# A hybrid decoder step on one core: the second layer's mixing four turns later, its loads left where they are

## The reference

```python
for l in range(DEPTH):                                   # DEPTH = 2
    sp, ss = adaln(c_prompt, ...), adaln(c_sample, ...)  # shift, scale, gate of each sub-layer
    hp = modulate(rmsnorm(xp, norm_mix[l]), sp[0], sp[1])
    if l % N_MIXERS == 0:
        mp, r_p = mla_prompt(hp, ...)                    # attention over the prompt
        ms, r_s = mla_sample(hs, pos_s, cache_mla[i], page_table, ...)   # 16 cached pages a sequence
    else:
        mp, st_p = pool_mixer(hp, zero_prefix, pos_p, w_pool[i], pool_scale[i])  # trailing means, a map
    xp = xp + sp[2][:, None, :] * mp
    hp = modulate(rmsnorm(xp, norm_ffn[l]), sp[3], sp[4])
    xp = xp + sp[5][:, None, :] * peer(hp, ...)          # and the same for the samples

def peer(h, w_q, subkeys, u, v):                         # per token, 8 heads
    s = einsum(q, subkeys); vals, idx = lax.top_k(s, 16) # two sides of 128 keys
    best, ci = lax.top_k(vals0 + vals1, 16)              # 16 of 256 pairs -> 16 experts of 16384
    a = gelu(einsum('td,tkd->tk', x, u[e]))
    return einsum('tk,tkd->td', softmax(best) * a, v[e])
```

## Time and profile before

| | |
|---|---|
| median of 3 runs | 3481.03 us (3477.01 to 3484.01) |
| the profiled execution: its own time | 3478.81 us |
| its span in the trace | 3477.0 us |
| mean granted TensorE clock | 0.883 |
| PE busy | 2769.2 us (80%) |
| DVE busy | 2276.8 us (65%) |
| ACT busy | 1038.8 us (30%) |
| POOL busy | 1211.8 us (35%) |
| read from HBM | 1260.46 MB, 364 GB/s over the span |

### The profile page before, as it was taken

One profiled execution on the slowest core, in us unless ns is written; L12 is line 12 of the kernel. 1 busy time (PEld: TensorE's weight loads), 2 busy tenths in 40 slices (PEclk: granted clock), 3 DMA queues, 4 the chain that ended last, 5 costly groups with the idle time before them and its releaser, 6 DMA issues.

```text
span 3477.0 us, 39434 instructions
## 1 busy us (share of the span) xinstructions
PE 2769.2 (80%) x11227; PEld 1231.0 (35%) x11227; DVE 2276.8 (65%) x6373; ACT 1038.8 (30%) x4428; POOL 1211.8 (35%) x1077
## 2 busy tenths in 40 slices
PE   4988889979889957988989769979875775666765
PEld 0345554434444423434434234434331232112321
DVE  1454558887877856777777576777776645565455
ACT  0222224424334412433435314434421111111111
POOL 0000014433333423443434334434444344444443
PEclk9989999989999978999999979999988677777777
DMA  9650049999999998999999989999999999999998
GB/s 338 253 207 24 13 182 406 407 364 409 376 375 413 404 354 358 416 401 408 409 397 410 417 337 414 412 405 419 403 391 411 410 422 409 421 406 372 421 421 353
DMA packets 201876, 1266.40 MB, mean 364 GB/s; under 512 B 23762, under 2 KB 44803, under 8 KB 61874
## 3 DMA queue, kind: packets, MB, share of 16 engines
q0 software_dynamic: 150784, 1091.03, 76.9%
q1 hardware_dynamic: 50873, 172.85, 13.1%
HBM read 1260.46 MB, written 3.79 MB: 364 GB/s over the span
## 4 chain that ended last, share of the span: by engine, by line
PE 40%; DMA 29%; DVE 15%; issue 7%; ACT 3%; POOL 2%; SPq 1%; DVEq 0%; POOLq 0%; ACTq 0%; PEldq 0%
PE bank L1106 15%; DMA ring<-in_uv,work 10%; DMA big<-in_uv,work 8%; DMA mod_mix<-in_uv,work 7%; PE bank L844 6%; PE bank L956 5%; DVE ring L1946 2%; DMA ring<-in_w_ada 2%; PE bank L861 2%; PE bank L790 2%; ACT work L1425 1%; PE bank L660 1%; PE bank L617 1%; PE bank L691 1%; POOL ring L1464 1%
## 5 line engine op out<-in xcount | busy, mean ns | idle before, releaser
L1106 PE MATMUL bank<-ring,work 128*64 128x512 f32 (+1 forms) x2080 | 909.3, 710 | 276.6 <-ACT work L1425 276.2
L1464 POOL DMA_INDIRECT ring<-in_uv,work x520 | 608.8, 1171 | 944.5 <-PE bank L1106 818.8
L1946 DVE CUSTOM_DVE_ANT_0 ring<-ring,mod_smp 128x1024 f32<-128x1024 f32 x512 | 622.3, 1224 | 273.2 <-DMA ring<-in_uv,work 266.4
L1413 ACT ACTIVATE work<-work 128x2 f32<-128x2 f32 x520 | 105.2, 202 | 1509.9 <-DVE work L1946 1509.6
L1464 POOL DMA_INDIRECT big<-in_uv,work x260 | 299.6, 1152 | 682.8 <-PE bank L1106 367.9
L844 PE MATMUL bank<-big 128*128 128x512 f32 x1024 | 512.1, 623 | 0.0
L1106 PE MATMUL bank<-big,work 128*64 128x512 f32 (+1 forms) x1040 | 317.7, 730 | 152.8 <-ACT work L1425 152.6
L1106 PEld LDWEIGHTS bank<-ring,work 128*64 128x64 f32 (+1 forms) x2080 | 211.2, 153 | 627.7 <-ACT work L1425 387.5
L1946 DVE CUSTOM_DVE_ANT_0 big<-big,mod_smp 128x1024 f32<-128x1024 f32 x256 | 309.8, 1224 | 138.9 <-DMA big<-in_uv,work 135.0
L1106 PE MATMUL bank<-work 128*64 128x512 f32 (+1 forms) x520 | 293.8, 693 | 93.6 <-ACT work L1425 93.5
L1425 ACT ACTIVATE work<-small,work 128x64 f32<-128x64 f32 (+1 forms) x1040 | 303.2, 339 | 145.2 <-DVE work L1956 139.1
(11 more groups left out here) (289 smaller groups left out, 3404.2 us busy)
## 6 DMA issues: line engine op xcount, KB each, us to landing
big<-in_wk SPq DMA_DIRECT2D x48, 1152.0 KB, 10.1
ring<-in_w_ada SPq DMA_DIRECT2D x64, 768.0 KB
work<-in_cache_mla SPq DMA_DIRECT2D x104, 160.0 KB, 8.9
ring<-in_uv,work POOLq DMA_INDIRECT x520, 11.8
big<-in_uv,work POOLq DMA_INDIRECT x260, 12.1
ring<-in_w_mla_out SPq DMA_DIRECT2D x1, 4096.0 KB, 13.0
big<-in_w_mla_out SPq DMA_DIRECT2D x4, 1024.0 KB, 11.6
mod_smp<-in_cache_mla SPq DMA_DIRECT2D x24, 160.0 KB, 12.7
```

Of the source, the lines that this page charges most:

```text
L1106: last = mm(out, diag[:, t % 2, j, 0:min(m, HALF)], s[:, D + half * 512:D + (half + 1) * 512], start=(k == 0 and (n < S0 or j == 0)), stop ...
L1413: act.activation(acts[:, t % 2 * GRP:(t % 2 + 1) * GRP], dots[:, t % 2 * GRP:(t % 2 + 1) * GRP], ACT.Gelu)\
L1464: pool.indirect_dma_start(slot[g % SLOTS], None, T["uv"].rearrange("l e d -> (l e) d"), bass.IndirectOffsetOnAxis(index[:, k * GRP + j:k * ...
L1946: dve.tensor_tensor_reduce(u, u, hb, 1.0, 0.0, ALU.mult, ALU.add, dots[:, at:at + 1]).then_inc(sem("dots_set"), 1)
```

## The change

Three numbers per pair are raised. The mixing (`mix_at`) and the norms after it (`norm_turn`) stand four turns later: 132 and 260, 140/142 and 268/270. The queries and the ranking of pairs 2 and 3 (`head_turn`) stand five turns later, and the loads of these pairs' first two heads (`t == opens + 12`) four. The loads of `mods` and `pooling_weights` keep their turns, since they are now counted from `opens` and not from `mix_at`. What is computed and what is loaded stays the same.

```diff
--- before.py
+++ after.py
@@ -289,7 +289,7 @@
         tile_of = lambda n: n % NT if n < S0 else NT
 
         def head_turn(q, h):
-            return (8 * h - 12 if h else -20, 54 + 9 * h, opens[2] + 19 + 12 * h, opens[4] + 19 + 12 * h)[q]
+            return (8 * h - 12 if h else -20, 54 + 9 * h, opens[2] + 24 + 12 * h, opens[4] + 24 + 12 * h)[q]
 
         PART_AT = ((0, 1, 2, 3, 4, 5, 6, 7), (0, 1, 2, 3, 4, 5, 7, 8), (0, 1, 2, 5, 6, 7, 10, 11), (0, 1, 2, 5, 6, 7, 10, 11))
         PARTS = ((0, 0), (0, 1), (0, 2), (1, 0), (1, 1), (1, 2), (0, 3), (1, 3))
@@ -306,9 +306,9 @@
         def rank_no(n, h):
             return n // 2 * 16 + h * 2 + n % 2 if n < S0 else 64 + n - S0
 
-        norm_turn = {0: -34, 1: -33, 2: 40, 3: 41, 4: opens[2] + 8, 5: opens[2] + 10, 6: opens[4] + 8, 7: opens[4] + 10,
+        norm_turn = {0: -34, 1: -33, 2: 40, 3: 41, 4: opens[2] + 12, 5: opens[2] + 14, 6: opens[4] + 12, 7: opens[4] + 14,
                      S0: smp_open[S0] + 2, S1: smp_open[S1] + 2}
-        mix_at = {4: opens[2], 6: opens[4]}
+        mix_at = {4: opens[2] + 4, 6: opens[4] + 4}
         ybank = lambda i: pb[4:6]
 
         busy = set(range(41, 46))
@@ -494,7 +494,7 @@
                         if h >= 2 and t == head_turn(q, h - 2) - 2:
                             sp.wait_ge(sem("sco_ps"), i - 1)
                             load_head(q // 2, i, h)
-                        if q and h < 2 and t == (40, opens[2] + 8, opens[4] + 8)[q - 1] + h:
+                        if q and h < 2 and t == (40, opens[2] + 12, opens[4] + 12)[q - 1] + h:
                             sp.wait_ge(sem("sco_ps"), q * PH)
                             if q >= 2:
                                 sp.wait_ge(sem("mix_w_free"), q - 1)
@@ -537,7 +537,7 @@
                 if t == 70:
                     w.next("mods_set")
                 for n in mix_at:
-                    if t == mix_at[n] - 2:
+                    if t == opens[n - 2] - 2:
                         sp.wait_ge(sem("choice_set"), n // 2 * 2 * PH)
                         mods(mod_pool, 1, 0, "prompt", P, T["norm_mix"][1], gain_pool)
                     if t == mix_at[n] + 2:
```

## The result

The kernel after the change takes 3493.11 us (median of 12 runs, 3485.01 to 3504.18), beside 3478.57 us of the kernel before (12 runs, 3472.63 to 3487.37): a ratio of 1.0038, 95% interval 1.0028 to 1.0048. By the ratio it is slower by 13 us, where 10 us less were forecast, and outside the range of 3456 to 3485. The profiled execution's own time is 3492.56 us (span 3490.8), 13.8 us over that of before.

What follows compares the result with a forecast made beforehand. The DMA engines were taken to bound the loop. Gains of 4.9 us (first mixing) and 4.4 (second), nothing for the ranking, together 9.3 off a median of 3481.0, gave 3472, taken as 3471 for the clock; range 3456 to 3485.

Steps and rivals of the forecast that it cites:

- The failed step: Ranking of two pairs, five turns later: same eight turns of every twelve, taken as nothing, within 3 us either way.
- this sign of being wrong: Whole loop: the prediction is wrong if stretches outside turns 129 to 143 and 257 to 271 differ more than these.
- The first mixing: `set_mods` at turn 133: DVE's wait shrinks from 27.4 to 14 us; gain 4.9 us, bounds -2.7 to 18.1.
- later idle time: PE in the first mixing, waiting for ACT: 7.5 us, taking up that much of its 10.4 us wait for `w_pool`.
- The second mixing: `set_mods` at turn 261: no wait for the pool scale, a page wait at turn 260; gain 4.4 us.
- the margin of 4: Second mixing: the pool scale, wanted at 2054.7, lands some 4 us after about 2047, so no wait.
- The forecast's term of 4.4 us: Second mixing: turn 272 starts at 2096.3 instead of 2100.7, a gain of 4.4 us.
- The bound of -5: Second mixing: lower bound of its gain, -5 us, for the pool scale landing late.
- The slower one: Rival at turn 265: pool scale lands late at 2072, 7.6 us lost there, kernel 10 us slower, 3491; chance 0.13.
- Hidden anyway: Rival for both mixings: transfers were hidden already, so the waits go and the time stays, 3480; chance 0.22.

Runs made afterwards that it cites:

- rank5: The kernel before with only the ranking and queries of pairs 2 and 3 five turns later, mixings unmoved: 3493.16 us against 3481.16, ratio 1.0043.
- early4: The changed kernel with the queries of head 4 of pairs 2 and 3 back in their old turns: 3480.03 us, ratio 0.9999 to the kernel before.
- mix4: The changed kernel with heads 1 to 7 of pairs 2 and 3 in their old turns, head 0 three turns later than before, ranked in nine: 3476.57 us, 0.9983.
- best: The kernel before with first mixing four turns later, head 0 of pair 2 at turn 150 ranked in nine, pool scale loaded before sequence 6's pages: 3469.4 us, 0.9968.
- scale1: The kernel before with the pool scale's load issued ahead of the 16 pages of sequence 6 instead of behind them: 3476.48 us, ratio 0.9981.
- before_w8: The kernel before with the loads of band and `w_pool` eight turns earlier: 3482.99 us, ratio 0.9992.
- rank7: The changed kernel with the ranking and queries of pairs 2 and 3 seven turns later than before instead of five: 3489.44 us, ratio 1.0015.

## Why the prediction was wrong

**The failed step** is the shortest one: "The ranking of two pairs stands five turns later ... I take nothing for it, within 3 us either way". It is worth +12 to +15 us: rank5 alone is at 1.0043 (3493.16 against 3481.16). That is a net figure. Taking six blocks of queries out of the shift brings the ratio from 1.0038 to 0.9977, about 18 to 21 us, for the shift also shortens turns 257 to 299 by 5 us (below). The prediction had named this sign of being wrong itself, the stretches outside the mixings differing more than those two. The step looked at what ranking is (the same eight turns of every twelve) and at how it falls on the sequences' tails, which is DVE's side. It never set the instructions that ranking issues on PE beside what stands next to them at their new place. The number that was missing is in the trace of before: PE busy 53.18 of 53.30 us under pages and ranking. A block of queries is 3.6 to 3.7 us, and 4.2 to 4.4 us of standing at each tile change (in the kernel before) come on top. With that row in view, the question "is PE late at turns 194 and 195?" asks itself.

The order of the loss, as far as the runs show it: ahead of the tile change PE has time to spare (6.4 us in the change), which is lost while the DMA engines are full; behind it PE is late by its wait and at a low clock, and all that stands there costs its length, for it delays L1106, which frees the slots. The four turns 194 to 197 took 8 us more than in early4, and 7.2 of them are queries; the rest may be the lower clock (0.89 against 0.96 in early4), which no run took apart.

**The first mixing** held. `norm_mix` was issued at 1268.29 and took 34.9 us (33.6 forecast); DVE waited 16.7 us (14). SP's and PE's entries, for the earlier trace rows:

```profile
1268.29 3.46 SPq L385 DMA_DIRECT2D big<-in_norm_mix  x1
...
1274.37 4.27 SPq L385 DMA_DIRECT2D big<-in_w_pool  x1
```

```profile
1315.97 3.38 PE L913 MATMUL bank<-big,hbuf 128*128 128x128 f32 x16 [4.31 <-DMA big<-in_w_pool]
...
1326.29 3.29 PE L1106 MATMUL bank<-big,work 128*64 128x512 f32 x8 [5.08 <-ACT work L1425]
```

`w_pool` landed 41.5 us after its issue, 47.0 were forecast, so PE waited 4.3 us for it and not 10.4, but of the 7.5 us of its later idle time 5.1 were left: the two errors are of opposite sign, 6.1 less and 5.1 more. The stretch took 109.6 us where 110.0 were forecast, which is closer than its parts were. mix4 and best, with 109.2 and 109.1, show that this gain is the shift's own.

**The second mixing** came out near its size by luck, and for another reason. The stretch took 95.1 us (93.8 forecast) and its waits are the ones named: PE stood 7.4 us for the page at turn 260 (3 to 8 forecast), and DVE 8.7 us at L1818 behind it (4.65 forecast):

```profile
2033.29 0.19 DVE L1818 TENSOR_SCALAR big<-bank 128x16 f32<-128x16 f32 x1 [8.71 <-PE bank L868]
```

and the scale, issued at 2040.28, landed 21.6 us later, 0.8 us after it was wanted (the margin of 4 was used up). But rank5, which leaves the mixing in place, has the same 95.0 us. Turns 257 to 271 alone can't settle it: with the ranking's shift they take 94.9 to 98.4 us (98.4 in early4), without it 96.0 to 98.1, scale1 and best left out for their own gain. Turns 257 to 299 can: 241.9 to 246.6 us in the six kernels with the shift, 247.9 to 250.0 in before, before_w8 and mix4. The mixing's own shift is worth next to nothing there, 250.0 to 249.3 us in mix4, and 244.7 in rank5 beside 245.0 in the change. So the gain of about 5 us comes with the ranking's shift. What in it brings the gain stays open: the queries of head 0 of pair 3 (7 us of PE's work) go from turns 269 and 270 to 274 and 275, which is still within these turns, and mix4 moves them to 272 and 273 and gains next to nothing. The forecast's term of 4.4 us for the mixing's own shift was a second step that failed: the scale's wait went, and the wait at L1818 and ACT's wait for L913 (two in mix4, 12.4 us in all) stand in its place. The bound of -5 that the prediction gives this term doesn't fit its own rival either, which works out to -7.6.

**The rivals.** None of them was the case. The slower one named the pool scale's landing, with a price near the loss (3491 us); it would be luck to count that as a hit, since that wait was 0.8 us. *Hidden anyway* holds for the second mixing alone.

## What to carry to other kernels

When a block of work is moved "five turns later", list its instructions on each engine and read what stands beside them at the new place, on the engine that frees the buffers first of all; a step that is costed at nothing needs such a row as much as one that is costed at five. Work that nobody is waiting for belongs ahead of a known stall and not behind it: in this kernel four blocks of 3.6 us filled a gap ahead of it and cost nearly their full length behind it (13 us). At one of the two tile changes two turns further behind was not far enough (rank7). And a late load was better cured here by its place in the queue (scale1: one line, 8.4 us of the stretch) than by moving those who wait for it (mix4: 0.7 us over turns 257 to 299).

## What the hardware showed beside this

The forecast let the two queues share the DMA engines packet for packet, as counted in the earlier trace rows, and the last of four 512 KB loads, issued behind 2.6 MB of pages, landed after 34.9 us, with 33.6 forecast. For `w_pool`, in rows of 1 KB, it was 41.5 us where 47.0 were forecast.

After PE's wait of 5.26 us at the tile change in the changed kernel the next eight matmuls of L1106 took 3.68 us and the next four of L844 3.78; some 15 us later they took 1.94 and 1.99. At turn 320 the same wait of 5.26 us was followed by the same 3.68 and 3.78. So both stalls were followed by work at about half speed, with a granted clock of 0.77 over turns 192 and 193 (1638.1 to 1647.2) and 0.89 over the next four. The Trainium skill (page "TensorE: Matmul & The Clock Gate", section "Part 1: The HAM clock gate (the "warmup" mystery)") says that PE has two levels, 1.2 and 2.4 GHz, and starts at the lower one after standing; these durations, 1.90 times as long, agree. What I had not expected is where it hurts: at the one place where PE has no time to give.
